# Three edits in the MLP chunks of a two-layer decoder trunk: wide matmuls first in each tile, the first stage's last product joined too, and one operand difference moved to GpSimd

## What is computed

```python
def _squared_relu_mlp(h, w1, w2):          # w1: 1024 x 4096, w2: 4096 x 1024
    return jnp.square(jax.nn.relu(h @ w1)) @ w2

for layer in range(2):
    h = _rms_norm(x, norm_mix_g[layer])
    x = x + mixer(h)                       # attention in layer 0, retention in layer 1
    h = _rms_norm(x, norm_ffn_g[layer])
    x = x + _squared_relu_mlp(h, ffn_w_in[layer], ffn_w_out[layer])
return _rms_norm(x, final_g)
```

## Time and profile before

| what | value |
| --- | --- |
| median of three runs | 1250.69 us |
| the profiled execution, its own time | 1250.86 us |
| its span in the profile | 1249.1 us |
| TensorE (matmuls) busy | 1238.4 us, 99% of the span |
| VectorE busy | 955.2 us, 76% |
| ScalarE busy | 768.6 us, 62% |
| GpSimd busy | 297.0 us, 24% |
| chain that ended last | TensorE 91%, VectorE 3%, DMA 2% |

### The profile page before, as it was taken

How to read it: one execution, slowest core, us unless ns; L and a number is a source line. 1 busy time by engine, 2 the same in 40 slices (tenths; PEclk the granted TensorE clock), 3 DMA queues, 4 the chain that set the end, 5 groups by cost and what they waited for, 6 DMA issues and landing times.

```text
span 1249.1 us, 18840 instructions
## 1 busy us (share of the span) xinstructions
PE 1238.4 (99%) x7158; PEld 1080.3 (86%) x7158; DVE 955.2 (76%) x1232; ACT 768.6 (62%) x1064; POOL 297.0 (24%) x330
## 2 busy tenths in 40 slices
PE   9999999999999999999999999999999999999997
PEld 6788888898898988989898889898889889898896
DVE  6588647599779697798666797567898967869678
ACT  6688755477564575665656645456667647456474
POOL 2343653111211112101231212231221122111220
PEclk9999999999999999999999999999999999999999
DMA  7367567788988989974968588879589899898992
GB/s 246 97 137 163 136 148 191 205 210 190 225 223 219 233 189 211 225 218 114 224 135 199 131 227 180 210 155 234 101 222 243 207 203 226 217 232 202 210 215 99
DMA packets 147978, 238.93 MB, mean 191 GB/s; under 512 B 51104, under 2 KB 72872, under 8 KB 147888
## 3 DMA queue, kind: packets, MB, share of 16 engines
q0 software_dynamic: 32352, 102.79, 43.8%
q1 hardware_dynamic: 115232, 134.60, 34.1%
q10 hardware_dynamic: 304, 0.33, 0.1%
HBM read 127.57 MB, written 2.11 MB: 104 GB/s over the span
## 4 chain that ended last, share of the span: by engine, by line
PE 91%; DVE 3%; DMA 2%; issue 1%; ACT 1%; POOL 0%; SPq 0%; POOLq 0%; DVEq 0%; ACTq 0%
PE banks L1042 21%; PE banks L1420 12%; PE banks L1010 11%; PE banks L1211 7%; PE banks L969 6%; PE banks L1488 6%; PE banks L1002 5%; PE banks L1370 5%; PE banks L1151 4%; PE banks L1005 2%; PE banks L1434 2%; PE banks L1312 2%; PE banks L1178 2%; PE banks L1384 1%; DMA raw_tiles<-raw_tiles 1%
## 5 line engine op out<-in xcount | busy, mean ns | idle before, releaser
L2294 DVE TENSOR_TENSOR w<-raw_tiles,w 128x1024 fp32r<-128x1024 f32 x312 | 371.1, 1220 | 55.7 <-ACT w L1630 55.4
L1630 ACT ACTIVATE w<-raw_tiles 128x1024 fp32r<-128x1024 f32 x312 | 315.2, 1051 | 123.7 <-PE banks L1042 61.9
L1042 PE MATMUL banks<-w,arena_q 128*128 128x512 f32 x1332 | 304.3, 390 | 0.0
L3283 POOL DMA_DIRECT2D raw_tiles<-raw_tiles x176 | 152.3, 907 | 629.1 <-DVE w L2294 378.6
L1042 PEld LDWEIGHTS banks<-w,arena_q 128*128 128x128 f32 x1332 | 249.3, 188 | 51.7 <-DVE x L2620 0.4
L1420 PE MATMUL banks<-w,h_ops 128*128 128x512 f32 x672 | 154.2, 390 | 0.0
L1420 PEld LDWEIGHTS banks<-w,h_ops 128*128 128x128 f32 x672 | 125.6, 188 | 25.7
L1010 PE MATMUL banks<-h_ops,w 128*128 128x256 f32 x1152 | 140.1, 283 | 0.0
L1010 PEld LDWEIGHTS banks<-h_ops,w 128*128 128x128 f32 x1152 | 139.4, 192 | 0.7
L1002 PE MATMUL banks<-h_ops,w 128*128 128x512 f32 x288 | 102.3, 400 | 0.1
L969 PE MATMUL banks<-h_ops,w 128*128 128x256 f32 x672 | 82.0, 284 | 0.0
(11 more groups left out here) (247 smaller groups left out, 1864.9 us busy)
## 6 DMA issues: line engine op xcount, KB each, us to landing
raw_tiles<-raw_tiles POOLq DMA_DIRECT2D x176, 512.0 KB, 5.6
raw_tiles<-in_ffn_w_in SPq DMA_DIRECT2D x64, 512.0 KB, 6.3
raw_tiles<-in_ffn_w_out SPq DMA_DIRECT2D x64, 512.0 KB, 6.4
raw_tiles<-in_odd_w_in SPq DMA_DIRECT2D x32, 512.0 KB, 5.5
raw_tiles<-in_even_w_in SPq DMA_DIRECT2D x48, 256.0 KB, 3.4
raw_tiles<-in_odd_w_in SPq DMA_DIRECT2D x32, 256.0 KB, 5.0
raw_tiles<-in_odd_w_out SPq DMA_DIRECT2D x16, 512.0 KB, 6.3
raw_tiles<-raw_tiles POOLq DMA_DIRECT2D x20, 256.0 KB, 4.1
```

Source lines behind the costliest of these rows:

```text
L1042: mm = pe.matmul(bank[first + t][:, :], a_ring[a_slot(g, i)][:, a, k, P * t:P * t + P], w_slots[use_slot(use)][:, b, k, :], start=(starts ...
L1630: nc.scalar.activation(w_flat(use_slot(use), 0, half), raws[tile][:, 1024 * half:1024 * half + 1024], ACT.Copy).then_inc(m_hi, 1)
L2294: nc.vector.tensor_tensor(w_flat(use_slot(use), 1, half), raws[use_tile(key)][:, 1024 * half:1024 * half + 1024], w_flat(use_slot(use), 0, ...
L3283: pool.dma_start(raws[dst][:, part], raws[src][:, part], accum_op=ALU.add).then_inc(t_made[value][half], 16)
```

## The change

1. `WIDE` gets product 6, so that the last product of the first stage is joined as well.
2. In a joined tile the four matmuls of 512 columns come first, for k = 0 to 3, and then the four of 256 columns.
3. As product 6 now lies in two halves, ScalarE copies its LOW half to SBUF (`last_copy`, two parts), VectorE adds its HIGH half (`wide_last`, two parts), and ScalarE applies ReLU to the sum (`wide_relu_last`, one operation of 1024 columns). S2 on VectorE comes later by two places.
4. In the six chunks S3 leaves VectorE's queue and goes to GpSimd's (`last_operand_sum`), behind the last weight sum (T4) of the second stage.

```diff
-WIDE = (1, 2, 3)
+WIDE = (1, 2, 3, 6)
@@ TensorE, wide_first_stage
+                        if i in WIDE:
+                            for k in range(4):
+                                if b == 0 and m == 0 and k % 2 == 0:
+                                    pe.wait_ge(m_lo, 2 * use + k // 2 + 1)
+                                pe.matmul(dst.rearrange("p (q n) -> p q n", q=2), w_slots[use_slot(use)][:, 0, k, c:c + P],
+                                          h_ops[:, H_BLOCK[op], :, k, :],
+                                          start=(i < 3 and k == 0), stop=(k == 3), skip_group_check=True)
+                            for k in range(4):
+                                mm = pe.matmul(dst[:, 0:256], w_slots[use_slot(use)][:, 1, k, c:c + P],
+                                               h_ops[:, H_BLOCK[op], 0, k, :],
+                                               start=False, stop=(k == 3), skip_group_check=True)
+                            continue
@@ ScalarE
+            def last_copy(g, b):
+                act.wait_ge(p_done, use_done(first_use(g, 6), b))
+                act.wait_ge(a_lo, 7 * g)
+                nc.scalar.activation(hidden_part(0, b, HIGH), wide_part(6, b, LOW), ACT.Copy).then_inc(last_copied, 1)
+            def wide_relu_last(g):
+                act.wait_ge(last_sum, wide_count(g) + 2)
+                block = a_blocks(1)["12"]
+                nc.scalar.activation(block, block, ACT.Relu).then_inc(last_relu, 2)
...
-                w_hi(stage + 1, 1, 0)
-                relu_last(g, 0)
-                w_hi(stage + 1, 1, 1)
-                relu_last(g, 1)
+                if g % CHUNKS:
+                    w_hi(stage + 1, 1, 0)
+                    last_copy(g, 0)
+                    last_copy(g, 1)
+                    w_hi(stage + 1, 1, 1)
+                    wide_relu_last(g)
@@ VectorE
+            def wide_last(g, b):
+                v = hidden_part(0, b, HIGH)
+                dve.wait_ge(last_copied, wide_count(g) + b + 1)
+                nc.vector.tensor_tensor(v, v, wide_part(6, b, HIGH), ALU.add).then_inc(last_sum, 1)
...
-                hidden_operand_sum(g, S2)
-                w_lo_both(stage + 1, 1)
+                if g % CHUNKS:
+                    w_lo(stage + 1, 1, 0)
+                    wide_last(g, 0)
+                    wide_last(g, 1)
+                    w_lo(stage + 1, 1, 1)
+                    hidden_operand_sum(g, S2)
...
-                hidden_operand_sum(g, S3)
+                if g % CHUNKS == 0:
+                    hidden_operand_sum(g, S3)
@@ GpSimd
+            def last_operand_sum(g):
+                a = a_blocks(1)
+                pool.wait_ge(s_made, sums_of(2 * (g // CHUNKS) + 1) + 4 * (g % CHUNKS + 1) + 3)
+                nc.gpsimd.tensor_tensor(a["21"], a["11"], a["21"], ALU.subtract).then_inc(s_made, 1)
...
                 for stage in range(first + 1, first + 2 * CHUNKS):
                     for value in (T1, T3, T2, T4):
                         weight_sum("mlp", stage, value)
+                    if stage % 2 and stage // 2 % CHUNKS:
+                        last_operand_sum(stage // 2)
```

More of the change, by code:

```diff
@@ L687, in trunk @@
         cross_added = [sem(f"cross_added{n}") for n in range(2)]
+        last_copied = sem("last_copied")
+        last_sum = sem("last_sum")
         m_square = sem("m_square")
@@ L1000, in wide_first_stage @@
                                 pe.wait_ge(m_lo, 2 * use + k // 2 + 1)
[L1001 to L1013, removed]
+                            for n, (p, q) in enumerate(PASSES):
+                                mm = pe.matmul(dst[:, 0:256], w_slots[use_slot(use)][:, p, k, c:c + P],
+                                               h_ops[:, H_BLOCK[op], q, k, :],
+                                               start=(i == 0 and k == 0 and n == 0), stop=(k == 3 and n == 2),
+                                               skip_group_check=True)
                     mm.then_inc(p_done, 1)
@@ L1688, in relu_last @@
                 act.wait_ge(p_done, use_done(first_use(g, 6), b))
[L1689 to L1692, removed]
+                act.wait_ge(hs_lo, 8 * (g // CHUNKS) + 4)
+                nc.scalar.activation(hidden_part(0, b, HIGH), pair_of(FIRST_X, b), ACT.Relu).then_inc(last_relu, 1)
+            def last_copy(g, b):
[6 more added lines that the diff above has]
+                nc.scalar.activation(block, block, ACT.Relu).then_inc(last_relu, 2)
             def square(g, n):
@@ L1757, in mlp @@
                 operand_hi(g, 1)
-                w_hi(stage + 1, 1, 0)
-                relu_last(g, 0)
-                w_hi(stage + 1, 1, 1)
-                relu_last(g, 1)
+                if g % CHUNKS:
[4 more added lines that the diff above has]
+                    wide_relu_last(g)
+                else:
+                    w_hi(stage + 1, 1, 0)
+                    relu_last(g, 0)
+                    w_hi(stage + 1, 1, 1)
+                    relu_last(g, 1)
                 square(g, 3)
@@ L2683, in mlp @@
                 operand_lo(g, 1)
-                hidden_operand_sum(g, S2)
-                w_lo_both(stage + 1, 1)
+                if g % CHUNKS:
[4 more added lines that the diff above has]
+                    hidden_operand_sum(g, S2)
+                else:
+                    hidden_operand_sum(g, S2)
+                    w_lo_both(stage + 1, 1)
                 if g % CHUNKS == 0:
```

## The result

The changed kernel takes 1266.55 us (median of 4 runs, 1266.43 to 1267.05) where the kernel before takes 1250.6 (4 runs, 1250.32 to 1250.83): ratio 1.0126, 95% interval 1.0113 to 1.0138. It is 16 us slower. Its profiled execution took 1267.05, with a span of 1265.2. The forecast was 1265.0, range 1257 to 1270.

The account below looks back on a forecast made before the run. TensorE bounds the kernel (91% of the chain), with VectorE 95% busy in second stages. Waits of 4 x 2.5 + 2.6 + 2.8 = 15.4, less 0.4, give +15.0 us on 1250.86: 1265.9, forecast 1265, range 1257 to 1270.

Parts of the forecast that it names:

- TensorE's part: Joined tiles and product 6: wide-first order and joining gain 0.07 us a chunk, 0.4 us in six.
- The chain behind product 6: Start of second stage: VectorE's `operand_lo(g, 2)` comes 2.01 us later, ending at 369.93 instead of 367.92.
- S3 leaving VectorE: VectorE's queue, second stage: S3's place is worth 1.14 us, leaving VectorE 0.87 us late.
- S3 on GpSimd: Behind T4's second DMA issue: S3 runs 2.25 us until 379.33, and VectorE's `w_lo` loses 2.2 us.
- exclusion: GpSimd and VectorE operations with two SBUF inputs block each other for the whole operation; PSUM adds are free.
- the first slot: S3's turn when `operand_lo(g, 3)` ends at 377.1: `w_lo` loses 2.2 us; leaned to, forecast 1265.
- What TensorE waits for: Second stages: products 3, 5 and 6 start 1.5, 2.2 and 2.5 us late; 15.4 us over six chunks.
- (1) No exclusion: S3 on GpSimd runs beside VectorE at no cost to the MLP: 1252.4 us; chance 0.10.
- (2) The gain arrives: All new work is hidden and TensorE's gain arrives in part or whole: down to 1249 us; chance 0.03.
- (3) A lucky slot: S3 falls beside several PSUM adds, losing about 0.6 us, or TensorE has more slack: 1254 to 1260; chance 0.07.
- the second slot: S3's turn at 378.2, beside `add_product(g, 1, 0)`: loss 1.6 us, time 1262.
- (4) The lag spreads: Loads behind T4 and next chunk's weights come late too, over 1 us more a chunk: 1271 to 1276; chance 0.05.

Follow-up runs that it names:

- experiment 3: Kernel before with only the matmul order in joined tiles changed (four of 512 columns, then four of 256), product 6 not joined: 1250.73 us, ratio 0.9996.
- experiment 8: Kernel before with new order and product 6 joined, but without the sum that joining needs; S3 on VectorE: 1250.44 us, ratio 1.0001.
- experiment 7: Changed kernel with S3 on VectorE and half of product 2's weights split in the wait ahead of `operand_lo(g, 2)`: 1252.88 us, ratio 1.0021.
- experiment 1: Changed kernel with S3 back in VectorE's queue behind `operand_lo(g, 3)`: 1260.04 us, ratio 1.007.
- experiment 4: Changed kernel with S3 on GpSimd computed for one column of 1024 only, waits and order kept: 1253.57 us, ratio 1.002.
- experiment 6: experiment 2 with four one-column memsets ahead of S3 on GpSimd: 1252.21 us, ratio 1.0017.
- experiment 2: Kernel before with S3 alone moved to GpSimd behind T4: 1256.35 us, ratio 1.004.
- experiment 5: Changed kernel with S3 on GpSimd computed for 512 of its 1024 columns: 1259.99 us, ratio 1.008.

## Why the prediction was right

**The whole.** Start-to-start times of TensorE give the difference by stages. The six second stages are longer by 2.68, 2.68, 2.84, 2.70, 3.04 and 2.38 us, together 16.32; products 1 to 3 of the six first stages are longer by 0.46 in all (0.04, -0.08, 0, -0.13, 0.23, 0.40); product 6 is shorter by 6 x 0.09 = 0.54. That is +16.2, as the two profiled executions differ (1250.86 and 1267.05). That it fits so closely is chance: outside these stretches 0.16 us are won ahead of chunk 1 and 0.28 in chunk 4, which the change doesn't touch, and 0.3 are lost behind the last second stage. Predicted were 15.4 - 0.4 = 15.0: the second stages lost 0.9 more than that, and the first stages won 0.1 instead of 0.4. Mechanism and path came out as forecast; the deviations are of size.

**TensorE's part.** Counted at 0.4 us, measured at nothing: experiments 3 and 8 each give no difference beyond the noise. A tile takes 1.40, as reckoned, but at product 3 of the first stage and at A11 TensorE meets a wait that takes it all. Both parts of the 0.07 a chunk, the 0.05 kept of product 6 and the rest from the order, came to nothing that can be measured.

**The chain behind product 6.** Predicted 2.01 us for `operand_lo(g, 2)`, at 369.93; measured at 369.88. Experiment 7 shows that the time lost is mostly VectorE's idle time ahead of it: work put there brings 7.2 of 9.4 us back.

**S3 leaving VectorE.** Its place was put at 1.14. Between experiments 1 and 4, where S3 is taken away and nothing is put in its place, the kernel gains 6.5 us, 1.08 a chunk.

**S3 on GpSimd.** The step that decided: exclusion, `w_lo` 2.2 us late. Measured 2.21 in each chunk, and 13.0 us between experiment 4 and the changed kernel. S3's turn was predicted until 379.33 and ended at 379.28. That is so close by luck, as two terms were wrong and cancel. S3 by itself takes 2.73 us (experiment 6, chunks 3, 6 and 7), not `split_lo`'s 2.40; and the start-up that passes while it waits is about 0.47, not 0.15, since its turn, counted from the end of `operand_lo(g, 3)`, lasts 2.26. The prediction had 2.40 - 0.15 = 2.25, the runs have 2.73 - 0.47 = 2.26. S3 was also ready 0.4 us sooner than reckoned (376.39, not 376.8), within the same slot, which closed at 377.03. That it took the first slot and not the second was called open. Experiments 2 and 6 show how near the two lie: four memsets of one column, 0.52 us together, decide between 2.6 to 3.0 us of delay and 1.6.

**What TensorE waits for.** Predicted +1.5, +2.2 and +2.5 at products 3, 5 and 6; measured 1.6 and 2.3 at products 3 and 5 and 2.7 by the stage's end. At product 6's start TensorE is 2.54 us late, as predicted; what the sum left out comes after it. In product 6 the second matmul starts 0.34 us behind the first, where the step is 0.227 else, and the stage ends 2.68 late: 0.15 a chunk. In chunk 6 another 0.36 is added from the wait at product 2 on. In chunk 7 the stage is 2.38 longer and 0.3 more is lost behind it, 2.7 against the 2.8 predicted. In all the six stages are 16.3 against 15.4. The waits at A11 and at product 2's weights (0.3 us together), which experiment 4 shows without S3, add nothing to this in the other chunks: TensorE waits at product 3 until VectorE's add is done, and they only shorten that wait.

**The rivals.** (1) No exclusion: excluded by the 3.43 us. Its time would have been 1253.6 (experiment 4) and not 1252.4: there the waits at A11 and at product 2 have no later wait that covers them. (2) The gain arrives: it doesn't, even alone (experiments 3, 8). (3) A lucky slot, beside several PSUM adds, for about 0.6: no run shows it. Experiment 6 gets the second slot, beside one PSUM add, for 1.6. (4) The lag spreads to the loads: a trace of it is there. ScalarE's `w_hi` waits 36.2 us in all for weight sums to land where it waited 17.3, and in the last two first stages TensorE waits 0.35 and 0.54 us at product 3, 0.6 more than before together. S3's place in GpSimd's queue isn't the whole cause: with S3 back on VectorE (experiment 1) the last first stage loses nothing, but that of chunk 6 still waits 0.44 there. The 0.42 us that chunk 6 loses at product 2 follow on 0.44 us in which VectorE stands still ahead of S4. They are in the changed kernel and in experiments 4 and 5, whatever S3's width, and in no run without S3 on GpSimd or without the longer chain (experiments 1, 2, 6, 7). So it appears only where both are there; how it comes about stays open.

## What to carry to other kernels

An operation of two SBUF inputs, moved from VectorE to GpSimd to relieve VectorE, can cost VectorE more than it takes there itself (here 2.2 against 1.14 us) if it meets an operation with two SBUF inputs. Look up in the timeline what VectorE runs at that moment: beside an add with an input from PSUM nothing was lost, and little decides which of the two it is (experiments 2 and 6). When a chain across engines grows, look for the idle time that it opens on the busiest of them and for work that can be put into it: that gave back 7 of 9 us here. A small wait can cost nothing where a later and longer one follows: the two at A11 and at product 2 vanished in the wait at product 3. And ask what the faster engine meets next before counting its gain.

## What the runs showed of the hardware

- A GpSimd operation that begins up to 0.34 us behind a VectorE operation of 1.2 us can still go first and hold it for its whole length (experiment 2, four of six meetings, each with another VectorE operation directly ahead). In experiment 6, with four memsets ahead of it, it never did, at 0.16 to 0.79 us behind. The recorded starts alone don't tell who wins; where the boundary lies, and what the memsets do to it, is open.
- A GpSimd operation that waits gets its turn between two VectorE operations that stand back to back (the changed kernel, six times); VectorE's queue doesn't shut it out. A VectorE operation held up ends 1.08 us behind GpSimd's end at both widths that held it up; 1.08 is short of the 1.22 of one undisturbed.
- A GpSimd subtraction of 1, 512 and 1024 columns takes 0.68, 1.78 and 2.89 us where it waits some 0.6 us for its turn, and then its first 0.68 cost VectorE nothing. Where it goes first (experiment 2) this doesn't hold: it takes 2.72 to 2.74 and VectorE loses 2.6 to 3.0.
- Matmuls of 512 columns behind some of 256 take 0.93 us for four, 0.233 each, against 0.227 in long runs; four of 256 behind them take 0.47, 0.118 each (experiment 3). In the second stages of the changed kernel, behind each wait of TensorE, the second matmul of 512 columns starts 0.31 to 0.34 us behind the first. The Trainium skill (TensorE: Matmul & The Clock Gate, section "Back-to-back issue gap") gives a sustained 131 ns for 512 columns; no run here comes near it, the fp32r matmuls of this kernel take 227 in long runs, at a granted clock of 1.00.
